# Normalisation sums in column strips, and a third projection tile in the gap between two layers

## What is computed

```python
for l in range(2):
    m = mixer(rmsnorm(h, norm_mix_pre[l]), w_in[l], ..., w_out[l])
    h = h + rmsnorm(m, norm_mix_post[l])
    f = swiglu(rmsnorm(h, norm_ffn_pre[l]), w_gate_up[l], w_down[l])
    h = h + rmsnorm(f, norm_ffn_post[l])
# rmsnorm(x, w) = x * rsqrt(mean(x*x over the 1024 columns) + eps) * w
```

## Time and profile of the kernel before

| | us |
|---|---|
| median of 3 runs (lowest, highest) | 1386.0 (1385.76, 1386.1) |
| the profiled execution, its own time | 1384.18 |
| its span, first to last instruction | 1382.4 |
| PE busy | 1362.3 (99%) |
| DVE busy | 1039.6 (75%) |
| ACT busy | 634.8 (46%) |

### The profile page before, as it was taken

One profiled execution on the slowest core, in us unless ns is written; L12 is line 12 of the kernel. 1 busy time (PEld: TensorE's weight loads), 2 busy tenths in 40 slices (PEclk: granted clock), 3 DMA queues, 4 the chain that ended last, 5 costly groups with the idle time before them and its releaser, 6 DMA issues.

```text
span 1382.4 us, 29088 instructions
## 1 busy us (share of the span) xinstructions
PE 1362.3 (99%) x12172; PEld 1339.7 (97%) x12172; DVE 1039.6 (75%) x1675; ACT 634.8 (46%) x1230; POOL 100.5 (7%) x141
## 2 busy tenths in 40 slices
PE   8999999999999999999999999999999999999997
PEld 8999999999999999999989999999999999999996
DVE  7746796768999898754586458968789989886545
ACT  5235554557545455422442364545575445454221
POOL 0001221000000000011000012110000000000110
PEclk9999999999999999999999999999999999999999
DMA  6332243122333333355413313321232333333552
GB/s 210 107 107 78 67 116 105 45 69 81 103 108 114 101 101 108 115 174 183 130 62 108 111 60 99 107 94 36 79 92 93 120 95 112 104 106 121 176 178 93
DMA packets 67491, 147.46 MB, mean 107 GB/s; under 512 B 20128, under 2 KB 23584, under 8 KB 67360
## 3 DMA queue, kind: packets, MB, share of 16 engines
q1 hardware_dynamic: 59536, 119.90, 27.3%
q0 software_dynamic: 7824, 25.70, 5.5%
HBM read 132.79 MB, written 12.78 MB: 105 GB/s over the span
## 4 chain that ended last, share of the span: by engine, by line
PE 88%; DVE 8%; ACT 1%; issue 1%; DMA 1%; SPq 0%; DVEq 0%; ACTq 0%
PE PS L676 48%; PE PS L1231 8%; PE PS L1232 8%; PE PS L1233 8%; PE PS L682 5%; DVE Wl L1875 1%; DVE hT L1913 1%; DVE Xl L1892 1%; DVE mT L1912 1%; PE PS L870 1%; DVE conv L2002 1%; PE PS L1197 1%; PE PS L1016 1%; PE PS L842 1%; PE PS L854 1%
## 5 line engine op out<-in xcount | busy, mean ns | idle before, releaser
L1310 ACT ACTIVATE Wh<-stage 128x1024 fp32r<-128x1024 f32 x143 | 151.1, 1058 | 327.6 <-PE PS L676 299.5
L676 PE MATMUL PS<-Xh,Wh 128*128 128x260 f32 x1376 | 285.5, 289 | 2.9 <-DVE Xl L1934 2.2
L676 PE MATMUL PS<-Xh,Wl 128*128 128x260 f32 x1376 | 277.0, 283 | 0.0
L676 PE MATMUL PS<-Xl,Wh 128*128 128x260 f32 x1376 | 276.5, 282 | 0.0
L1875 DVE TENSOR_TENSOR Wl<-stage,Wh 128x1024 fp32r<-128x1024 f32 x143 | 174.6, 1222 | 105.7 <-ACT Wh L1310 105.0
L676 PEld LDWEIGHTS PS<-Xh,Wh 128*128 128x128 f32 x1376 | 211.4, 189 | 6.5 <-DVE Xl L1934 2.6
L676 PEld LDWEIGHTS PS<-Xh,Wl 128*128 128x128 f32 x1376 | 211.8, 188 | 0.0
L676 PEld LDWEIGHTS PS<-Xl,Wh 128*128 128x128 f32 x1376 | 211.7, 188 | 0.0
L1231 PE MATMUL PS<-XU,hiA 128*128 128x260 f32 x448 | 126.8, 283 | 0.0
L1231 PE MATMUL PS<-XU,hiB 128*128 128x260 f32 x448 | 126.8, 283 | 0.0
L1232 PE MATMUL PS<-XU,hiB 128*128 128x260 f32 x448 | 126.6, 283 | 0.0
(11 more groups left out here) (384 smaller groups left out, 2865.8 us busy)
## 6 DMA issues: line engine op xcount, KB each, us to landing
stage<-w_slabs SPq DMA_DIRECT2D x143, 512.0 KB, 3.3
raw<-w_slabs SPq DMA_DIRECT2D x136, 256.0 KB, 3.0
dst<-state_ret POOLq DMA_DIRECT2D x32, 256.0 KB, 3.8
dst<-state_gdn POOLq DMA_DIRECT2D x32, 256.0 KB, 3.8
out_gdn_sample<-dst POOLq DMA_DIRECT2D x16, 256.0 KB, 3.0
out_ret_sample<-dst POOLq DMA_DIRECT2D x16, 256.0 KB, 3.5
hT<-x_t SPq DMA_DIRECT2D x3, 520.0 KB, 6.5
out_y_t<-hT SPq DMA_DIRECT2D x3, 520.0 KB, 3.0
```

The source lines that it names most:

```text
L676: ins = mm(pj(slot)[:, a], w[:, ws, pos, :], x[:, a, :], start=first and w is Wh and x is xh, stop=last and w is Wl)
L1310: A(Wh[:, G % NW], stage[:, G % NS], ACT.Copy).then_inc(s["hi_split"], 1)
```

## The change

* **Strips.** At `n` = 2 and, between the layers, at `n` = 0, four blocks' squares are summed by four matmuls with only 32 columns of ones, each into its own strip of 32 partitions of one bank (`strip_sums`). After two such groups (first half) or one (second half, `n` = 0) ACT copies the bank to SBUF, scaled by 1/32 (`strips_copied`), and one full matmul of ones adds the strips (`strips_added`). In the second half at `n` = 0 blocks 4 to 7 still get full matmuls (`rest_sums`).
* **Buffers.** Each square has its own place (`sq0`, `sqb0`, `sqb1`), so ACT's squares wait for no sum.
* **ACT's order in `second_x`.** `strips_copied` of the first half after the rounding of block 4, that of the second half (`n` = 0) after block 6; the first half's `root_mean` moves from after block 3 to after block 7.
* **Slab 2.** Its `hi` moves from after the first half's squares to just after the rounding of block 4; its `lo` from after `second_half_x` to before it.
* **Third tile, between the layers.** Tile 2 moves from `proj` to `first_halves`: its first half block by block along with the second half of tiles 0 and 1, its second half after the gate columns. In layer 1 it uses banks 6 and 7 and the gate columns bank 4, after the first half's `rb`.

```diff
+            def strip_sums(l, n, a, k0, last):
+                pe.wait_ge(s["xsq_ready"], nth_square(l, n, k0 + 3, a))
+                for j in range(4):
+                    rows = rows_at(j, QB)
+                    ins = mm(PS[rows, 4 + a, 0:HC], ones[:, 0:QB], (sq0 if n else (sqb0, sqb1)[a])[:, k0 + j, :], start=k0 == 0, stop=last, skip_group_check=True)
+                if last:
+                    ins.then_inc(s["x_sums"], KT - 1 if k0 else KT // 2)
+            def strips_added(l, n, a):
+                pe.wait_ge(s["xsq_ready"], part_at(l, n, a))
+                return mm(PS[:, 4 + a, 0:HC], ones, part2[:] if n else part0[:, a], start=True, stop=n == 2 or a == 0)
+            def rest_sums(l, k0, k1):
+                pe.wait_ge(s["xsq_ready"], nth_square(l, 0, k1 - 1, 1))
+                for k in range(k0, k1):
+                    mm(PS[:, 5, 0:HC], ones, sqb1[:, k, :], start=False, stop=k == KT - 1).then_inc(s["x_sums"], 1)
...
                     for a in range(2):
                         for k in range(KT):
                             pe.wait_ge(s["x_ready"], nth_norm(l, n) + nth(l, n, k, a))
-                            if k and not (n and a):
-                                add_sums(l, n, k - 1, a)
-                            if k == KT - 1 and not (n and a):
-                                add_sums(l, n, k, a)
+                            if a == 0 and k == 5:
+                                strip_sums(l, n, 0, 0, False)
+                            if a and k == 2:
+                                strip_sums(l, n, 0, 4, True)
+                            if a and k == 6:
+                                strips_added(l, n, 0).then_inc(s["x_sums"], 1)
...
+                            if a and n == 0:
+                                third(k, 0)
+                            if a and n == 0 and k == 4:
+                                strip_sums(l, n, 1, 0, True)
+                            if a and n == 0 and k == KT - 1:
+                                strips_added(l, n, 1)
+                                rest_sums(l, 4, KT)
...
+                    else:
+                        gate_columns()
+                        for k in range(KT):
+                            third(k, 1)
...
+                def gate_columns():
+                    pe.wait_ge(s["wba_ready"], l + 1)
+                    if l:
+                        pe.wait_ge(s["rb_ready"], l * 8 + 1)
...
+                def strips_copied(n, a, l):
+                    act.wait_ge(s["x_sums"], nth_norm(l, n) + (KT + KT // 2 if a else KT - 1))
+                    A(part2[:] if n else part0[:, a], PS[:, 4 + a, 0:HC], ACT.Copy, scale=1.0 / QB).then_inc(s["xsq_ready"], 1)
                 def second_x(n, l=l):
+                    if n == 0:
+                        act.wait_ge(s["tile_done"], l * TILES)
                     for k in range(KT):
                         round_x(n, k, 1, l)
+                        if k == 4:
+                            strips_copied(n, 0, l)
                         if k:
                             second_square(n, k - 1, l)
-                        if k == 3:
+                        if k == 7:
                             root_mean(n, 0, l)
+                        if n == 0 and k == SUM_AT:
+                            strips_copied(0, 1, l)
                     second_square(n, KT - 1, l)
...
                     for k in range(4, KT):
                         round_x(0, k, 0, l + 1)
                         square_x(0, k - 1, 0, l + 1)
+                        if k == 4:
+                            hi(G0 + SLABS + 2)
                         if k == 5:
                             root_mean(3, 1)
                     square_x(0, KT - 1, 0, l + 1)
-                    hi(G0 + SLABS + 2)
                     second_x(0, l + 1)
...
                 if l + 1 < DEPTH:
+                    lo(G0 + SLABS + 2)
                     second_half_x(3, l + 1)
-                    lo(G0 + SLABS + 2)
```

More of the change, by code:

```diff
@@ L196, in trunk @@
         sq2 = at("sq2", A0, o, [P, KT, HC])
+        sq0 = at("sq0", A0, o + KT * HC, [P, KT, HC])
+        part2 = at("part2", A0, o + 2 * KT * HC, [P, HC])
         PT = at("PT", A0, o + NC * U, [P, NC, H, P])
@@ L269, in trunk @@
         assert (FT + 2) * HF <= ROWS and ROWS + 12 * P <= XU_N
+        sqb0 = at("sqb0", A0, ROWS, [P, KT, HC])
+        sqb1 = at("sqb1", A0, 0, [P, KT, HC])
+        part0 = at("part0", A0, KT * HC, [P, 2, HC])
+        assert ROWS + KT * HC <= XU_N
         PS = ctx.enter_context(nc.psum_tensor("PS", [P, 8, 512], fp32))
@@ L356, in rows_at, with slot_of, gate_bank @@
             return slice(i * n, (i + 1) * n)
-        def slot_of(t):
-            return t if t < 3 else (t + 1) % 2
+        def slot_of(t, l=0):
+            return 3 if t == 2 and l else t if t < 3 else (t + 1) % 2
+        def gate_bank(l):
+            return 4 if l else 6
         def banks(slot):
@@ L438, in trunk @@
         SPLIT = KT - 2 + 1
+        SUM_AT = 6
         def nth(l, n, k, a):
@@ L454, in nth_norm, with nth_square, part_at @@
             return (l * 2 + n // 2) * HN
+        def nth_square(l, n, k, a):
+            at = nth_norm(l, n) + l + 2 * (l if n else max(l - 1, 0))
+            if l == 0 and n == 0:
+                return at + 2 * (k + 1)
+            return at + a * KT + k + 1 + ((a and k >= 3) + (n == 0 and a and k >= SUM_AT))
+        def part_at(l, n, a):
+            return nth_square(l, n, SUM_AT - 1 if a else 2, 1) + 1
         def wait_free(eng, G):
@@ L1017, in products @@
                     ins.then_inc(s["kq_mm"], 1)
+                def gate_columns():
+                    pe.wait_ge(s["wba_ready"], l + 1)
+                    if l:
+                        pe.wait_ge(s["rb_ready"], l * 8 + 1)
+                    for j in range(0, KT, 2):
+                        for i in range(2):
+                            for a in range(2):
+                                rows = slice((2 * a + i) * BA_M, (2 * a + i + 1) * BA_M)
+                                ins = mm(PS[rows, gate_bank(l), 0:HC], wbs[:, j + i, :], hT[:, j + i, a, :], start=j == 0, stop=j == KT - 2, skip_group_check=True)
+                    ins.then_inc(s["ba_done"], 1)
                 if l == 0:
                     first_two()
+                    gate_columns()
                 else:
+                    at_step[0] += KT
                     first_halves(0, 0, 0)
[L1024 to L1031, removed]
+                proj(3 * KT if l == 0 else 2 * KT)
                 pe.wait_ge(s["badiag_ready"], l + 1)
@@ L1318, in square @@
                     if n % 2 == 0:
[L1319 to L1329, removed]
-                    else:
[L1331 to L1338, removed]
+                        A(sq0[:, k] if n else (sqb0, sqb1)[a][:, k], src, ACT.Square).then_inc(s["xsq_ready"], 1)
+                        return
+                    if n == 1 and h and k >= 4:
+                        act.wait_ge(s["out_sums"], l * (KT - 3) + k - 3)
+                    elif k >= 2:
+                        act.wait_ge(s["sq_added"], nth_added(l, n, k - 2, 1 if a is None else a))
+                    elif n == 1:
+                        act.wait_ge(s["st_mm"], (l + 1) * H)
+                    else:
+                        act.wait_ge(s["x_sums"], nth_norm(l, n) + HN)
                     to = sqh[:, k % 2] if a is None else sqh[:, k % 2, a]
@@ L2083, in _ @@
                         done(t)
-                        step.go(V.tensor_tensor(halves(rT[:, t, :]), pj(slot_of(t))[:, :, 0:HALF], rb[:, :, 0:HALF], ALU.mult))
-                        freed(V.tensor_tensor(halves(rD[:, t, :]), pj(slot_of(t))[:, :, HALF:HC], rb[:, :, HALF:HC], ALU.mult), t)
+                        step.go(V.tensor_tensor(halves(rT[:, t, :]), pj(slot_of(t, l))[:, :, 0:HALF], rb[:, :, 0:HALF], ALU.mult))
+                        freed(V.tensor_tensor(halves(rD[:, t, :]), pj(slot_of(t, l))[:, :, HALF:HC], rb[:, :, HALF:HC], ALU.mult), t)
                     elif t < 4 * H:
@@ L2114, in _ @@
                             rows = half_rows(a)
-                            step.go(V.tensor_tensor(ba[rows], PS[rows, 6, 0:HC], rb[rows, a], ALU.mult))
+                            step.go(V.tensor_tensor(ba[rows], PS[rows, gate_bank(l), 0:HC], rb[rows, a], ALU.mult))
                         step.need()
```

28 lines of the change are left out of this document (13 added, 15 removed).

## The result

The changed kernel took 1391.4 us (median of 5 runs, 1390.0 to 1392.6) beside 1386.0 for the kernel before (5 runs, 1384.6 to 1386.3): ratio 1.0043, 95% interval 1.0033 to 1.0054. It is slower by 5.4 us, 2.5 more than the forecast and just past the top of its range (1391.0). A later, longer comparison of the same two kernels gave 1390.1 (11 runs) against 1385.8 (32 runs), 4.3 us more, ratio 1.0030 (1.0021 to 1.0039), which lies inside the forecast's range.

A forecast was written before the change was run, and what follows sets the result against it. It took DVE's and ACT's chain to `Xl` to bound the stretch ahead of the SwiGLU, and a mixed chain between the layers. 2 x 0.44 + 2.0 = +2.9 us took the median from 1386.0 to 1388.9; range 1385.5 to 1391.0.

The forecast's parts named there:

- step 3: Between the layers: PE restarts on block 1 at 699.6; with strip groups at 0.47 block 7 could begin at 707.5.
- the fallen clock: Rival, between the layers: PE stands, its clock falls to 1.2 GHz, up to 6 us more; chance 0.05.
- SwiGLU: Ahead of each SwiGLU: removed sums gain nothing, the added sum costs +0.44; twice, +0.9; bounds 0 to 0.6 each.
- Steps 1 and 2: Between the layers: slab 2's moved `hi` (+0.94) and `lo` (+1.13) put `Xl` of the second half's block 0 at 697.1.
- Step 4: Between the layers: second half's copy awaits first half's added sum, block 7's rounding queues behind; block 7 at 708.1, PE stands 0.6.
- Steps 5 and 6: Between the layers: logarithm at 711.65 (+4.6); tile 3 waits for slab 3's `lo` and starts at 717.45 (+2.0).
- A reading that was wrong: Whole kernel: nearly all PE waits, away from the start, lie in the three short stretches the change touches.
- the low end of its range: 1385.5, for a stretch between the layers that gains half a microsecond beside a SwiGLU part at half its price.

The follow-up runs named there:

- gap filled: The changed kernel plus 18 matmuls that nobody reads in PE's gap between the layers: 1388.3 us, ratio 1.0023 to the kernel before.
- repeat: The changed kernel run once more with no edit: 1390.1 us, ratio 1.0030 to the kernel before.

## Why the prediction missed

The forecast was +2.9 us, slower, on the line of what can be told; it came out +5.4 in the first comparison and +4.3 in the longer one. Direction and mechanism held. Two terms failed: step 3, which took a strip group at 0.47 us where it costs 0.77, and the fallen clock, which stood outside the sum with a chance of 0.05 and came in every profile that had the gap open, at 0.6 to 1.5 us. Point by point, times of the runs brought to those of the kernel before by the start of slab 1's `hi`:

| step | predicted | change (clock falls) | gap filled |
|---|---|---|---|
| 2. `Xl` of block 0, second half | 697.1 | 697.05 | 697.03 |
| 3. PE on block 1 | 699.6 | 699.7 | 699.5 |
| 4. added sum | 705.95 | 707.2 (repeat: 708.0) | 706.56 |
| 4. block 7 | 708.1 | 709.2 | 708.56 |
| 5. logarithm | 711.65 | 712.8 | 712.13 |
| 6. tile 3 | 717.45 | 718.6 | 717.96 |

* **SwiGLU, right.** +0.44 each, only the added sum on the path; 2.14 us of PE work ahead of 333.96 gave nothing.
* **Steps 1 and 2, right** to 0.15 us: DVE's wait for ACT (0.67 ahead of the first half's block 6), `lo` ahead of the second half, `Xl` a microsecond later.
* **Step 3, the term that was mis-sized.** Two strip groups at 0.47 cost 0.77 each where they stand, more than the 0.6 of its upper bound. The prediction saw 0.09 on entering the strips, put 0.2 to 0.4 for two groups into its range, and left it out of the sum. The 0.47 came from 16 matmuls in a row; four alone take 0.58, with 0.09 ahead and 0.10 behind. That is the 0.6 by which even the filled gap is late at the added sum. The Trainium skill, TensorEngine Tiling (Array Packing), section Tiling Modes, says that a change of mode drains the engine. The traces agree with that for the 0.09 ahead of a group, since the added sum, a full matmul, has no such delay (709.95 to 710.06). The 0.10 behind it is no sign of it: it follows a plain wait as well (712.06 to 712.29).
* **The rival that was given too little.** The prediction had foreseen PE's gap at 2.7 us (it came to 2.4 from the end of one matmul's 0.12 to the next start) and gave a falling clock 0.05, as a separate case of up to 6 us more. Its grounds were that the trace had no such gap behind the start, and that at half busy the clock had stayed 1.00; but that row is busy 1.50 of 2.00 us, and PE's wait there was 0.95, so it says little on a gap of 2.4. The clock fell in each of the five profiles that had the gap with nothing in it, and there in none of the nine whose waits were shorter (0.95 at most) or whose gap was filled. But it cost 0.6 to 1.5 us and not 6: it lasted some 3 us, and part of it fell into time that PE would have waited for `Xl`. It should have been a term of the sum.
* **Step 4, right.** The ring from added sum to block 7 took 2.0 us (2.15 predicted). **Steps 5 and 6, right**: 3.57 from block 7 to the logarithm (3.55), 5.83 from there to tile 3 (5.8).
* **A reading that was wrong.** Not nearly all of PE's waits behind the start lie in the three stretches: in the kernel before some 3 us do and some 4 us lie elsewhere, 1.1 of them the wait for `bv`. The forecast does not hang on it. Nor do the words for the low end of its range give 1385.5: half a microsecond won and half of 0.9 lost from 1386.0 make 1385.95.
* **What had no step.** The start of the program. It differs by up to 2 us from profile to profile; of 14 the six with gate columns from 24.2 to 24.8 had the clock down to 0.50 to 0.53 in one of the windows between 11 and 15 us, the others (22.7 to 23.6) had it at 1.00. The profile of the changed kernel had the late one, that of the kernel before the early one. What decides the start is not settled: the code there is the same in all, and both kinds occur with the change and without the part of it between the layers.
* **The first set's 1.35 us more than the longer set's, open in part.** The record has the mean granted clock of every run. In the kernel before, the 27 of 94 runs at 0.998 took 1384.8 us on average, the 33 at 0.996 took 1386.0. Two profiles with a late start and no fall between the layers have 0.996, so the kernel before probably has such starts too. The changed kernel's first five runs all had 0.996 or less; of its eleven later ones two had 0.998 and took 1388.75 both. So part of the 1.35 goes with a lower clock, though where it fell in runs without a profile is not known; at equal clock the first set is still 0.4 to 0.8 slower, and the cause of that stays open.

With 0.6 for the strips and 0.6 to 1.5 for the clock the sum would have been 1390.1 to 1391.0, at whose lower end the longer set lies. The first set's 1391.4 lies above it.

## What to carry to other kernels

Before removing work from the busiest engine, find the last wait in the stretch: what stands ahead of it is free already, and what a cheaper scheme moves behind it is paid in full. A rearrangement that lets TensorE stand as long as it did here should be charged with a fallen clock behind the gap, as a term of the sum and not as an unlikely case beside it. The price of a small group of matmuls is taken from where it will stand, with what it adds to the matmuls on both sides.

## What the hardware showed

* Behind a gap of 2.3 us in PE's timeline the granted clock fell to 0.50 for about 3 us, in five profiles of five, within a program that was busy 98% of the time. With 18 matmuls of no use in the gap it stayed at 1.00, and tile 3 came 0.6 to 1.5 us earlier.
* PE's busy time hides this: a window at half clock is busy 2.00 of 2.00 us, with 12 matmuls in it instead of 19.
* An idle time in PE's timeline understates what its removal wins, by some 0.2 us each time: 0.33 and 0.90 shown, 0.6 and 1.1 won.
* Four fp32 matmuls of 260 columns into four strips, alone between full matmuls, cost 0.77 us; 16 in a row cost 0.47 for each four.
